# The last expert job written out: its rows added on chip by a 0/1 product, the other rows gathered under it, and the first block of rows split

## What is computed

```python
logits = h @ w_router + b_router ; probs = softmax(logits)
top_p, top_i = top_k(probs, 2) ; top_p = top_p / sum(top_p)
for e in range(8):
    y = y + gates[..., e:e+1] * ((silu(h @ wg[e]) * (h @ wu[e])) @ wd[e])
x = x + rmsnorm(y, g_post_ffn)
```

## Time and profile before

| | us |
|---|---|
| median of 3 runs (1871.5 to 1873.53) | 1872.14 |
| the profiled execution, its own time | 1870.68 |
| its span, first to last instruction | 1868.9 |
| mean granted TensorE clock | 0.947 |

### The profile page before, as it was taken

One profiled execution on the slowest core, in us unless ns is written; L12 is line 12 of the kernel. 1 busy time (PEld: TensorE's weight loads), 2 busy tenths in 40 slices (PEclk: granted clock), 3 DMA queues, 4 the chain that ended last, 5 costly groups with the idle time before them and its releaser, 6 DMA issues.

```text
span 1868.9 us, 28900 instructions
## 1 busy us (share of the span) xinstructions
PE 1703.2 (91%) x11238; PEld 1537.5 (82%) x11238; DVE 950.4 (51%) x1140; ACT 732.7 (39%) x959; POOL 535.0 (29%) x326
## 2 busy tenths in 40 slices
PE   6899787899999997889899997999999999999991
PEld 5898587899999997889565494889898998989881
DVE  6796535211111004231684516767686675857764
ACT  6354443222222123121454223345454444544543
POOL 1001232355554342231000021343241423315242
PEclk9899888999999998999899998899999999999996
DMA  6533202144445232122534215769779696987934
GB/s 209 111 96 114 68 23 68 46 140 140 140 140 186 85 130 89 46 90 69 199 123 133 78 35 146 239 214 286 201 235 248 198 297 195 260 222 229 259 110 154
DMA packets 345379, 282.65 MB, mean 151 GB/s; under 512 B 9585, under 2 KB 309661, under 8 KB 345175
## 3 DMA queue, kind: packets, MB, share of 16 engines
q1 hardware_dynamic: 325619, 253.45, 46.3%
q10 hardware_dynamic: 16532, 16.57, 2.6%
q0 software_dynamic: 3168, 11.80, 2.1%
HBM read 247.40 MB, written 35.10 MB: 151 GB/s over the span
## 4 chain that ended last, share of the span: by engine, by line
PE 44%; issue 27%; POOL 12%; DVE 11%; ACT 4%; DMA 1%; SPq 1%; POOLq 0%; ACTq 0%; DVEq 0%
PE ps L2172 33%; POOL ea L838 9%; DVE cT L1511 2%; PE ps L2300 2%; POOL ea L840 1%; DVE wlo L1388 1%; PE ps L2134 1%; DVE rstd L1353 1%; PE ps L2124 1%; PE ps L2197 1%; DVE zc L1830 1%; PE ps L2541 1%; PE ps L2310 1%; PE ps L2490 1%; ACT zc L1163 1%
## 5 line engine op out<-in xcount | busy, mean ns | idle before, releaser
L2675 PE MATMUL ps<-ejx,ewh 128*128 128x384 f32 x1408 | 402.5, 360 | 2.7 <-issue 1.9
L2014 DVE TENSOR_TENSOR ewl<-eraw,ewh 128x2048 fp32r<-128x2048 f32 (+1 forms) x144 | 303.9, 2111 | 183.1 <-ACT ewh L1266 182.8
L1266 ACT ACTIVATE ewh<-eraw 128x2048 fp32r<-128x2048 f32 (+1 forms) x144 | 255.3, 1773 | 297.1 <-PE ps L2678 165.3
L2678 PE MATMUL ps<-ejx,ewl 128*128 128x192 f32 x1408 | 353.4, 251 | 0.0
L2172 PE MATMUL ps<-hh,whi 128*128 128x260 f32 x1504 | 317.2, 293 | 39.0 <-DVE hl L1744 27.5
L2172 PE MATMUL ps<-hh,wlo 128*128 128x260 f32 x1504 | 309.7, 288 | 0.0
L2172 PE MATMUL ps<-hl,whi 128*128 128x260 f32 x1504 | 309.6, 288 | 0.0
L838 POOL TENSOR_TENSOR ea<-eat,ea 128x128 fp32r<-128x128 f32 x88 | 181.7, 2065 | 424.4 <-ACT ea L1301 424.4
L2172 PEld LDWEIGHTS ps<-hh,whi 128*128 128x128 f32 x1504 | 241.6, 195 | 43.1 <-issue 30.0
L2678 PEld LDWEIGHTS ps<-ejx,ewl 128*128 128x128 f32 x1408 | 269.8, 192 | 0.0
L2675 PEld LDWEIGHTS ps<-ejx,ewh 128*128 128x128 f32 x1408 | 264.4, 188 | 6.3 <-issue 6.3
(11 more groups left out here) (393 smaller groups left out, 2619.3 us busy)
## 6 DMA issues: line engine op xcount, KB each, us to landing
eraw<-in_w_gate_e SPq DMA_DIRECT2D x88, 512.0 KB, 4.6
eraw<-in_w_up_e SPq DMA_DIRECT2D x88, 512.0 KB, 5.9
eraw<-in_w_down_e SPq DMA_DIRECT2D x64, 512.0 KB, 5.8
eraw<-in_w_down_e SPq DMA_DIRECT2D x48, 256.0 KB, 2.7
xs<-zero ACTq DMA_DIRECT2D x10, 1152.0 KB, 4.8
raw<-in_w_gate_d SPq DMA_DIRECT2D x22, 512.0 KB, 3.9
raw<-in_w_up_d SPq DMA_DIRECT2D x22, 512.0 KB, 5.1
raw<-in_w_down_d SPq DMA_DIRECT2D x16, 512.0 KB, 4.3
```

Of the source, the lines that this page charges most:

```text
L1266: e.activation(ewh[:, s, 0:n], eraw[:, u % RAW, 0:n], ACT.Copy).then_inc(ew_hi, 1)
L2014: e.tensor_tensor(ewl[:, s, 0:n], eraw[:, u % RAW, 0:n], ewh[:, s, 0:n].bitcast(F32), ALU.subtract)\
L2675: e.matmul(ps[:, q, 0:2 * C], ewh[:, s, o:o + P], ejx[:, k, :, :].rearrange("p h n -> p (h n)"), start=(k == 0), stop=(k == KD - 1), skip_ ...
L2678: ins = e.matmul(ps[:, q, C:2 * C], ewl[:, s, o:o + P], ejx[:, k, 0, :], start=False, stop=(k == KD - 1), skip_group_check=True)
```

## The change

- **First block split.** ScalarE makes the high part of the normed rows (`hth`), VectorE the low part (`row_low`, `htl`); `oh` becomes a plain 0/1 matrix, and TensorE adds the fp32r products of both parts, tile by tile. Its banks are opened by products with zeros (`open_rows`).
- **Order on VectorE.** `row_out` of all five tiles moves behind the first weight split and into job 0: two ahead of `first_rows_lo`, one ahead of step 0, one in step 1 and one in step 2. The gate weights move behind job 0, followed by eleven new linked steps and fifteen 0/1 matrices (`ohm`, `ohd`) for the last job.
- **Waits for the scatters.** SyncE's wait for `xs_in` moves from ahead of weight load 6 to behind weight load 7; GpSimd's goes to the last job; ScalarE's from step 2 to step 5.
- **Rows turned by tile height.** In `rows_in` the eight transposes of 128 rows come first, then the eight of 64 rows.
- **Last job written out.** The loops run to `last`, the number of jobs less one, and the last job follows as code of its own. In place of `rows_in` TensorE turns the 0/1 matrices (`selection`). The job before it is stored during step 9's loads; GpSimd gathers rows behind its tiles 3 to 6 and behind its last; ScalarE and VectorE weight, add and split them during the down projection. A use that lies in the last block is sent to a row with weight 0.
- **Tail.** The last job's result is scaled and split straight out of its banks (`eyh`, `eyl`), and TensorE puts each tile together: 4 matmuls that open it with the gathered sum and 8 that add the last job's rows. Square, root, norm and residual follow as before, but the tile of 8 comes last.

The diff, cut to its core, each engine's lines moved to the left:

```diff
@@ SP @@
-e.wait_ge(xs_in, 160)
...
     if u == 7:
         e.wait_ge(er_done, 4)
+        e.wait_ge(xs_in, 160)
         load_rows(2)
...
-e.wait_ge(ey_ready, nj * 4 + 4)
-store_rows(nj)
...
+    if u == 9:
+        e.wait_ge(ey_ready, nj * 4)
+        store_rows(last)
...
+e.wait_ge(f_dve, FD[f"out{NT}"])
+e.dma_start(y_sample.rearrange("b s d -> (b s) d"), fw[0:B, NT, :]).then_inc(y_out, 16)
@@ POOL @@
-e.wait_ge(xs_in, 160)
...
+with e.Fori(0, last) as j:
...
+        rest(j, m)
+for m in range(KE):
+    if m == 3:
+        e.wait_ge(er_done, nj * 4)
+        e.wait_ge(ys_out, nj * 32 + 16)
+        e.wait_ge(xs_in, 160)
+        e.wait_ge(last_ready, 1)
+    if m == KE - 1:
+        e.wait_ge(eg_done, nj * (2 * KE))
+    rest(last, m)
+    if 3 <= m <= 6:
+        row_back(m - 3, 0)
+        row_back(m - 3, 1)
+row_back(NT, 0)
+row_back(NT, 1)
@@ ACT @@
+e.wait_ge(rr, RR_RS)
+for i in range(NT + 1):
+    n = P if i < NT else B
+    e.activation(hth[i][0:n, :], xtk[0:n, i, :], ACT.Copy, scale=r5[0:n, 10, i:i + 1]).then_inc(rr_act, 1)
 e.wait_ge(rt_step, RT_M1)
-e.activation(rt[:, 6, :, :], rt[:, 2, :, :], ACT.Exp).then_inc(rr_exp, 1)
...
-        if first and u == 2:
+        if first and u == 5:
             e.wait_ge(xs_in, 160)
...
+        if u == 9 or u == 10:
+            early_one(u - 9)
+        if u == KE:
+            selection(last)
+            early_one(2)
+            e.preload_act_table(ACT.Sqrt)
         if u == KE + 1:
-            for c in range(4):
-                rows_hi(c, j * 4 + (4 + c + 1))
+            early_one(3)
+            early_one(4)
+        if u == KE + 2 or u == KE + 3:
+            early_hi(2 * (u - KE - 2))
+            early_hi(2 * (u - KE - 2) + 1)
+        if u == KE + 4:
+            early_hi(4)
@@ DVE @@
+def row_low(i):
+    n = P if i < NT else B
+    e.wait_ge(rr_act, i + 1)
+    e.scalar_tensor_tensor(out=htl[i][0:n, :], in0=xtk[0:n, i, :], scalar=rs[0:n, i:i + 1],
+                           in1=hth[i][0:n, :].bitcast(F32), op0=ALU.mult, op1=ALU.subtract).then_inc(first_dve, 1)
+row_low(0)
...
 for i in range(NT + 1):
     n = P if i < NT else B
-    e.tensor_scalar(oh[0:n, i, :], colf[0:n, :], own_slot[0:n, i:i + 1], rs[0:n, i:i + 1],
-                    ALU.is_equal, ALU.mult).then_inc(oh_ready, 1)
...
+for i in range(1, NT + 1):
+    row_low(i)
...
-e.wait_ge(rr_exp, 1)
...
+def early_sum(i):
+    n = P if i < NT else B
+    e.wait_ge(f_act, FA[f"one{i}"])
+    e.scalar_tensor_tensor(out=fo[i][0:n, :], in0=fs1[i][0:n, :], scalar=gme[0:n, 1, i:i + 1],
+                           in1=fo[i][0:n, :], op0=ALU.mult, op1=ALU.add).then_inc(f_dve, 1)
+def early_lo(i):
+    n = P if i < NT else B
+    e.wait_ge(f_act, FA[f"hi{i}"])
+    e.tensor_tensor(flo[i][0:n, :], fo[i][0:n, :], fhi[i][0:n, :].bitcast(F32),
+                    ALU.subtract).then_inc(f_dve, 1)
...
+            if first and 1 <= u <= 2:
+                row_out(u + 2)
         if u == 1:
             result_rows(j + 1, j * 32 + 16, j * 2 + 2)
...
 expert_lo(0, 0)
-expert_lo(0, 1)
+e.wait_ge(gf_in, 16)
+row_out(0)
+row_out(1)
+e.wait_ge(jobs_ready, 1)
 nj = e.value_load(jobi[0:1, MAXJOBS:MAXJOBS + 1], min_val=E, max_val=MAXJOBS)
 for c in range(4):
     first_rows_lo(c)
-expert_dve(0)
-with e.Fori(1, nj) as j:
+expert_lo(0, 1)
+row_out(2)
+expert_dve(0, True)
...
+link(e.tensor_scalar(lbase, jobf[:, MAXJOBS:MAXJOBS + 1], float(C), -float(C), ALU.mult, ALU.add))
+link(e.tensor_tensor(own_last, slf[:, 0, :], slf[:, 1, :], ALU.max))
+link(e.tensor_scalar(own_last, own_last, lbase, None, ALU.subtract))
...
+link(e.tensor_tensor(gate_last, tle[:, 0, :], tle[:, 1, :], ALU.add))
+link(e.tensor_tensor(gme[:, :, :], gate[:, :, :], tle[:, :, :], ALU.subtract))
+for i in range(NT + 1):
+    n = P if i < NT else B
+    e.tensor_scalar(ohm[0:n, i, :], colf[0:n, 0:P], own_last[0:n, i:i + 1], None, ALU.is_equal)
+    for h in range(2):
+        ins = e.tensor_scalar(ohd[i][0:n, CB * h:CB * h + CB], colf[0:n, P:C], own_last[0:n, i:i + 1], None, ALU.is_equal)
+ins.then_inc(last_ready, 1)
...
+last = e.value_load(jobi[0:1, MAXJOBS + 1:MAXJOBS + 2], min_val=E - 1, max_val=MAXJOBS - 1)
+with e.Fori(1, last) as j:
...
+expert_lo(last, 0)
+expert_lo(last, 1)
+expert_dve(last, last=True)
...
+for k in range(4):
+    c, n = k // 2, k % 2
+    e.wait_ge(f_act, FA[f"y{k}"])
+    e.scalar_tensor_tensor(out=eyl[:, c, 512 * n:512 * n + 512], in0=ps[:, 2 + k, :], scalar=gsl[:, c:c + 1],
+                           in1=eyh[:, c, 512 * n:512 * n + 512].bitcast(F32), op0=ALU.mult, op1=ALU.subtract)\
+     .then_inc(f_dve, 1)
@@ PE @@
+open_rows(0)
+open_rows(1)
...
+open_rows(2)
+open_rows(3)
...
+def first_rows(part, i, c):
...
+        ins = e.matmul(ps[:, q, k * C:(k + 1) * C], (hth[i][0:n, d], htl[i][0:n, d])[part], oh[0:n, i, :],
+                       start=False, stop=(part == 1 and i == NT), skip_group_check=True)
+    return ins
...
+    for i in range(NT + 1):
+        if c == 0:
+            e.wait_ge(first_dve, FIRST_LOW[i])
+        ins = first_rows(1, i, c)
     ins.then_inc(er_done, 1)
 zero_rows(3).then_inc(ed_done, 1)
...
+    for c in range(4):
+        q = EB[eb_at(2 * KE + c)[0]]
+        for k in range(2):
+            kk = 2 * c + k
             ins = e.transpose(ps[:, q, k * C + P:(k + 1) * C], gtok[0:CB, 1, kk * P:(kk + 1) * P],
                               ident[0:CB, 0:CB])
         ins.then_inc(er_done, 1)
...
+def selection(j):
+    e.wait_ge(last_ready, 1)
+    for c in range(4):
+        q = EB[eb_at(2 * KE + c)[0]]
+        eb_wait(j, 2 * KE + c)
+        if c == 3:
+            for h in range(2):
+                for i in range(NT + 1):
+                    n = P if i < NT else B
+                    e.matmul(ps[:, q, 256 + h:257 + h], (ohm[0:n, i, :], ohd[i][0:n, :])[h], gate_last[0:n, i:i + 1],
+                             start=(i == 0), stop=(i == NT), skip_group_check=True)
+        for i in ((0, 1, 2), (3, 4))[c % 2]:
+            n = P if i < NT else B
+            o = P * (i % 3)
+            ins = e.transpose(ps[:, q, o:o + n], (ohm[0:n, i, :], ohd[i][0:n, :])[c // 2], ident[0:n, 0:n])
+        ins.then_inc(er_done, 1)
...
+def open_tile(i):
+    n = P if i < NT else B
+    b = F_BANKS[i]
+    for part, (s, at_) in enumerate(((f_act, FA[f"hi{i}"]), (f_dve, FD[f"lo{i}"]))):
+        e.wait_ge(s, at_)
+        v = (fhi[i], flo[i])[part]
+        for h in range(2):
+            e.matmul(ps[0:n, b + h, :], eye[0:n, 0:n], v[0:n, 512 * h:512 * h + 512], start=(part == 0), stop=False,
+                     skip_group_check=True)
...
+def add_rows(i, part):
+    n = P if i < NT else B
+    b = F_BANKS[i]
+    for k in range(4):
+        c, h = k // 2, k % 2
...
+        ins = e.matmul(ps[0:n, b + h, :], sel[:, c, i * P:i * P + n], (eyh, eyl)[part][:, c, 512 * h:512 * h + 512],
+                       start=False, stop=(part == 1 and c == 1), skip_group_check=True)
+    return ins
+open_tile(0)
+open_tile(1)
+add_rows(0, 0)
+add_rows(1, 0)
+add_rows(0, 1).then_inc(f_pe, 1)
+add_rows(1, 1).then_inc(f_pe, 1)
+for i in range(2, NF):
+    if i == NT:
+        e.wait_ge(f_dve, FD["w0"])
+    open_tile(i)
+    add_rows(i, 0)
+    add_rows(i, 1).then_inc(f_pe, 1)
```

More of the change, by code:

```diff
@@ L2081, in _ @@
                 first_rows_lo(c)
-            expert_dve(0)
-            with e.Fori(1, nj) as j:
+            expert_lo(0, 1)
+            row_out(2)
+            expert_dve(0, True)
+            e.wait_ge(rr_act, RR_EXP)
+            link(e.tensor_reduce(zs, pr, AX, ALU.add))
+            link(e.reciprocal(zs, zs))
+            link(e.tensor_tensor(pr, pr, over_e(zs), ALU.mult))
+            link(e.tensor_tensor(dl, pr, oh1, ALU.mult))
+            link(e.tensor_reduce(p1, dl, AX, ALU.add))
+            link(e.tensor_tensor(dl, pr, oh2, ALU.mult))
@@ new lines, in _ @@
+            e.wait_ge(gp_in, 16)
+            for i in range(NF):
+                n = P if i < NT else B
+                b = F_BANKS[i]
+                e.wait_ge(f_act, FA[f"root{i}"])
+                e.reciprocal(frs[0:n, i, 1:2], frs[0:n, i, 1:2]).then_inc(f_dve, 1)
+                e.wait_ge(f_dve, FD[f"inv{i}"])
+                e.scalar_tensor_tensor(out=fw[0:n, i, :], in0=ps[0:n, b:b + 2, :].rearrange("p b n -> p (b n)"),
+                                       scalar=frs[0:n, i, 1:2], in1=gpost[0:n, :], op0=ALU.mult, op1=ALU.mult).then_inc(f_dve, 1)
+                e.wait_ge(f_dve, FD[f"w{i}"])
+                e.tensor_tensor(fw[0:n, i, :], fw[0:n, i, :], xtk[0:n, i, :], ALU.add).then_inc(f_dve, 1)
@@ L2614, in _, with open_rows @@
                 zero_rows(c)
+            copied_out(e, TP_XT + 8)
+            copied_out(e, TP_XT + 9)
+            copied_out(e, TP_LG)
+            def open_rows(c):
+                q = EB[eb_at(2 * KE + c)[0]]
+                e.matmul(ps[:, q, 0:256], ones[:, :], zero[:, 0:256], start=True, stop=False, skip_group_check=True)
```

(8 more changed lines are left out.)

256 lines of the change are left out of this document (145 added, 111 removed).

## The result

The changed kernel takes **1846.18 us** (median of 4 runs, 1845.12 to 1849.65) against 1871.82 (1869.76 to 1873.53) for the kernel before: a ratio of 0.9867, 95% interval 0.9850 to 0.9884. The prediction was 1849.7 in a range of 1840 to 1860, faster.

A forecast was written before the change was run, and what follows sets the result against it. TensorE, busy 91% of the span, was taken to bound the jobs, with idle time in the tail and a slow first block. Terms summed to -22.4, from 1870.7 to 1848.3 profiled, median 1.5 higher: 1849.7, range 1840 to 1860.

The forecast's parts named there:

- First block: Ahead of job 0: VectorE's chain sets the start, so job 0 starts at 1180.7 in place of 1189.7, -9.0 us.
- Job 0, GpSimd: Start of job 0: late row tiles and scatters delay GpSimd's first low tile, so step 6 starts late, +1.7 us.
- Job 0, SyncE: Job 0: weight load 8 queues behind the scatter wait and row load, so step 8 is late, +2.9 us.
- Between job 0 and 1: Job boundary: VectorE's gate weights, new steps and 0/1 matrices delay job 1's first low part, +5.4 us.
- Clock: Ahead of job 0 and at the boundary to job 1: one low clock spell of 1.6 each, +3.2 us.
- Rows turned: Row transposes by height: 1.4 us saved in each of seven jobs, -9.8; two low clock spells gone, -3.2.
- Last job: Last job: `selection` takes 4.2 for 3.7 us, +0.5; gathers make ScalarE's high parts of steps 15 to 17 late, +1.5.
- Tail: Behind the last down matmul: store, gathers and weighting go, leaving 22.4 in place of 38.0 us, -15.6.
- Sum: Whole kernel: all forecast terms together, -22.4 us, from 1870.7 to 1848.3 profiled, with the median at 1849.7.
- the head's gain stays: Rival: some 8 of the 13.2 us of stalls and clock losses don't come, giving 1841.7; chance 0.15.
- The gathers are not hidden: Rival: eight GpSimd gathers in steps 5 to 8 take 2 us, not 1; end some 8 later, 1857.7; chance 0.18.
- The clock stays low: Rival: half clock persists ahead of job 0, at the boundary, in last job and tail, costing 29.6: 1876.1; chance 0.04.

The follow-up runs named there:

- a_first: Changed kernel with VectorE making the first two scattered row tiles behind the first block's low parts and the second operand: 1844.74 us, ratio 0.9859.
- b_fill: Kernel before with zero products on TensorE before and after the products of the routing counts: 1864.22 us, ratio 0.9955.
- a_whole: Changed kernel with its first block in full 32-bit records again, not split into two parts: 1847.10 us, ratio 0.9867.
- a_row4: Changed kernel with VectorE's last row tile (8 rows) made in step 1 of job 0 in place of step 2: 1841.64 us, ratio 0.9841.
- a_sp: Changed kernel with SyncE's wait for job 0's last scatter, and the row load after it, behind weight load 10 in place of 7: 1841.99 us, ratio 0.9850.
- a_one4: Changed kernel with the last job's ScalarE copy of the eight-row tile, and VectorE's sum, in step 15 in place of 12: 1842.28 us, ratio 0.9850.
- a_gates: Changed kernel with VectorE's gate weights, last-job slots and small 0/1 matrices spread over job 0's down projection: 1837.50 us, ratio 0.9828.
- a_all: Changed kernel with the edits of a_sp, a_gates and a_one4 together: 1829.42 us, ratio 0.9789.
- a_alt: Changed kernel with the rows of a job turned in alternating tile heights again, as before: 1866.56 us, ratio 0.9960.

## Why the prediction was right, step by step

**First block: forecast -9.0, measured -11.6 from the routing.** The bound was named rightly: TensorE waits 2.96 for `first_rows_lo`, and a_first moves the start with VectorE's chain. "Even at the low clock" did not come: the changed kernel multiplies zero rows around the counts, the clock stayed up, and the 80 products took 10.6 us, not 13. But TensorE was not the bound, so this by itself moved nothing. What was sized too long is VectorE's chain, by 2.6: its first step on the counts comes 1.2 sooner behind the routing, since their products ran at full clock (1.26 us for 2.28), the 0/1 matrices took 1.23 for 1.63, and the pieces behind them are 1.0 shorter in sum. Along the experiments the 11.6 come apart as 8.3 clock (b_fill), 1.8 split (a_whole) and 1.5 between those two kernels (22.02 - 20.47). These 1.5 are all in the 80 full products (16.1 and 14.6); the stretches ahead of them and behind them are equal.

**Job 0, GpSimd: forecast +1.7, measured about 0.5** (a wait of 0.34 where the usual is none, and a longer step). The mechanism is the forecast one, as a_row4 shows. The sizes are not: two scatters were issued in 4.1 us and the first low tile took 0.8, not 2.4. The forecast's own pieces (1200.5, two scatters of 1 to 2 and 2.4) end at 1206.9 at the latest, not at 1208.5, so its 1.7 does not follow from them.

**Job 0, SyncE: forecast +2.9, measured 1.95.** Step 8 as forecast, for the reason forecast (a_sp). SyncE's wait ended at about 1207.6, where 1207 was said. The size is luck: an operand ready at 1219.5 for a step due at 1218.6 is 0.9 late, not 2.9, and 282 and 399 GB/s change the 1.8 MB ahead by 1.9 us, not by 6. In the profile ScalarE had load 8 at 1216.39, later than the 1214 forecast, and the operand was ready at 1221.1.

**Between job 0 and 1: forecast +5.4, measured 5.74 - 0.30 = 5.4.** Here 7.4 us of VectorE work were priced at 7.8.

**Clock: forecast +3.2, measured some 7.** Spells came at the start of job 0, behind the wait of step 8, in job 1 and behind `selection`, four of about 1.7 in place of two of 1.6. The step that failed is the list of places: each idle time that the prediction found for itself (step 8, the last job) should have been given a spell too. Which of them comes varies from one execution to the next: in a_one4's profile, whose job 0 is the same code, the two spells of job 0 are missing. That job takes 87.87 in place of 89.62, so both together cost 1.75 and not 3.4: without them TensorE waits longer, 2.00 ahead of step 8 and 1.26 in the turned rows. The 7 is what the slow products took; the time lost by them is less where other waits stand beside them.

**Rows turned: forecast -9.8 and -3.2, measured -12.2 and -4.2.** Too dear were the 1.0 for the rows of 64, where eight took 0.71, and the changes of height. The wait for the last bank came as forecast, on the weight load:

```profile
1237.52 0.20 PEld L2816 LDWEIGHTS ps<-ident,gtok 128*128 128x128 f32 x2 [0.26 <-DVE eup L2134]
```

1.74 per job, not 1.4. Of the 4.2, 3.2 are the two spells that are gone; the 1.0 of job 1 (slow steps at full clock) went with this execution and is not shown to be an effect of the edit.

**Last job: forecast +0.5 and +1.5, measured about +0.3 and +2.1**, and a spell of 1.7. `selection` took 4.03 for the forecast 4.2. The waits came in the steps named, behind the ScalarE wait named.

**Tail: forecast -15.6, measured -15.7.** 22.31 for 22.4; VectorE's last row ends 19.9 behind the end of the last down matmul, where 19.7 was said:

```profile
1828.45 0.16 DVE L2247 RECIPROCAL frs<-frs 128x1 f32<-128x1 f32 x1 [2.90 <-ACT frs L1427]
...
1840.55 1.21 DVE L2252 TENSOR_TENSOR fw<-fw,xtk 8x1024 f32<-8x1024 f32 x1
```

**Sum: forecast -22.4, measured -24.9 in span and -26.9 from the routing.** The terms that were off lie on both sides: first block 2.6 and turned rows 3.4 too small a gain, the clock 3.7 too small a loss, and the stalls of job 0 2.2 too large. That is 11.9 us of errors of which 4.5 are left over, so the nearness of 1849.7 to 1846.2 is in part their cancelling; the tail and the piece between job 0 and 1 are forecasts that held by themselves. **The rivals:** "the head's gain stays" fell, since 8 us of stalls and two spells did come. "The gathers are not hidden" fell: the eight gathers beside tiles 3 to 6 took 0.94 to 1.01 us each to issue, no matmul of those steps waited for their results, and the only waits that the gathers caused came from the place of one ScalarE copy (a_one4). "The clock stays low" fell: the first block, where it had its strongest row, is where the clock was won back.

## What to carry to other kernels

Look at the cheapest edit of a diff on its own: here the order of 16 transposes, repeated in each job, gave two thirds of the gain, while two thirds of what the two large rebuildings won (27 us) was lost again beside them (18 us). Put an instruction that waits for another engine as late in its queue as its result allows, and spread a long piece of small steps over a stretch where its engine has room: two such waits (a_sp, a_one4) and one such piece (a_gates) were worth another 13 us together. And where TensorE idles ahead of a dense stretch, look at the granted clock of that stretch before its instructions: eight of the twelve us of the first block were clock, not work.

## What the runs showed that was not expected

**Zero products hold the clock.** With idle stretches ahead of the block cut from 2.7 and 2.5 us to 1.4 and 1.0, the clock stood at 1.00 where it had been 0.50. In the kernel before it had already fallen when the first idle stretch (1156.75 to 1159.44) ended. The window and the counts there, then the counts of the changed kernel:

```profile
1159.00:1170.00 11.00, 8.04 (x27) 7.10 (x28) 8.89 (x26) 3.71 (x2) 4.72 (x4) 0.50 0.25 103
```

```profile
1159.89 2.28 PE L2619 MATMUL ps<-rt,ones 128*128 128x40 f32 x10
```

```profile
1161.66 1.26 PE L2770 MATMUL ps<-rt,ones 128*128 128x40 f32 x10
```

So the first idle stretch was enough for the fall. What the second one adds was not run.

**Alternating heights cost TensorE most of a short matmul.** A pair of transposes (128 and 64 rows) took 0.46 in turn, and (1.46 + 0.71)/8 = 0.27 in order of height. The short ones are narrower too (64 columns), so it is not shown whether height or width does it.

**GpSimd's indirect DMA took three times as long to issue beside VectorE's weight split.** GpSimd at the start of job 0 in the changed kernel, then VectorE there:

```profile
1178.38 0.97 POOL L862 DMA_INDIRECT xs<-htok,sloti  x1 [0.30 <-issue]
1179.66 3.13 POOL L862 DMA_INDIRECT xs<-htok,sloti  x1 [0.30 <-issue]
```

```profile
1177.07 2.69 DVE L2112 SCALAR_TENSOR_TENSOR ejx<-ps,gT,ejx 128x192 fp32r<-128x192 f32 x8
1179.67 2.28 DVE L2098 TENSOR_TENSOR ewl<-eraw,ewh 128x2048 fp32r<-128x2048 f32 x1
```

The first issue lies beside an instruction that reads PSUM, the second beside one that reads SBUF twice. All three issues of about 3 us in this kernel (3.13, 3.10, 2.93) begin within 0.12 us of such a subtraction, and the other seven took 0.85 to 1.19. In the kernel before, issues beside the same subtraction took 0.95, 1.90 and 1.86, and those beside `row_out`, which reads SBUF twice as well, 2.07 once and then 0.95 three times. So two SBUF operands alone do not explain it, and the cause stays open.

**Not settled.** In one or two jobs of some profiles (job 1 of the kernel before, of b_fill, a_gates and a_all; jobs 3 and 5 of a_alt) the gate and up steps take 4.64 us in place of 4.55 at clock 1.00, 1.0 us per job; the cause was not looked for. The 80 full products took 16.1 us in b_fill and 14.6 in a_whole, both at clock 1.00; in b_fill ten GpSimd instructions lie beside them and in a_whole four, but nothing was run to tell that from the order of the products. And why the routing starts up to 6 us sooner or later from one execution to the next was not followed.
